# Two compressed first layers in one step, projections moved up, and an output projection that opens with the convolution's half

## The reference, cut to what matters

```python
proj = h @ w_in                       # q, six k/v parts, gate logits, b_gate, c_gate, u
k_c = rms_norm(compress(kv[0], ...)); v_c = compress(kv[1], ...)
# compress: 32-token blocks with stride 16 -> silu(blocks @ w1) @ w2; w1 is 2048 x 256
o_attn = g0 * attention(k_c, v_c) + g1 * attention(k_s, v_s) + g2 * attention(k_w, v_w)
y_conv = b_gate * short_conv(c_gate * u, conv_w)      # width 3 over tokens
mix = rms_norm(concat([o_attn, y_conv]) in groups of 64)
x = x + g1 * (mix @ w_out)
h2 = rms_norm(x) * (1 + sc2) + sh2
x = x + g2 * hier_moe(h2)             # 64 experts, two per token
```

## Time and profile before

| | |
|---|---|
| median of 3 runs | 1448.33 us (1446.87 to 1449.07) |
| profiled execution, whole time | 1447.13 us |
| its span | 1445.3 us |
| mean granted TensorE clock | 0.872 of full |
| busy: PE / PE weight loads | 1028.2 us (71%) / 532.5 us (37%) |
| busy: DVE / ACT / POOL | 457.4 us (32%) / 166.1 us (11%) / 59.1 us (4%) |
| DMA | 503.75 MB, mean 349 GB/s |

### The profile page before, as it was taken

One profiled execution on the slowest core, in us unless ns is written; L12 is line 12 of the kernel. 1 busy time (PEld: TensorE's weight loads), 2 busy tenths in 40 slices (PEclk: granted clock), 3 DMA queues, 4 the chain that ended last, 5 costly groups with the idle time before them and its releaser, 6 DMA issues.

```text
span 1445.3 us, 14719 instructions
## 1 busy us (share of the span) xinstructions
PE 1028.2 (71%) x5933; PEld 532.5 (37%) x5933; DVE 457.4 (32%) x932; ACT 166.1 (11%) x409; POOL 59.1 (4%) x94
## 2 busy tenths in 40 slices
PE   4999999999999986466465664665645646566366
PEld 1867688655455442122121221212212212122121
DVE  1255477443467361121120211212112112021121
ACT  1132222012233210000000000000000000000000
POOL 4000210011020000000000000000000000000000
PEclk9999999999999999788887887878868878788688
DMA  9946656656626579999999999999999999999996
GB/s 352 370 169 239 240 219 233 230 95 204 225 85 243 205 296 428 428 428 428 427 429 428 429 428 428 429 429 428 429 429 429 429 429 428 429 429 427 428 426 260
DMA packets 78638, 503.75 MB, mean 349 GB/s; under 512 B 5318, under 2 KB 10718, under 8 KB 54020
## 3 DMA queue, kind: packets, MB, share of 16 engines
q1 hardware_dynamic: 75872, 496.22, 83.8%
q0 software_dynamic: 2656, 6.93, 2.1%
q10 hardware_dynamic: 68, 0.02, 0.0%
HBM read 501.54 MB, written 1.61 MB: 348 GB/s over the span
## 4 chain that ended last, share of the span: by engine, by line
PE 50%; DMA 41%; DVE 4%; SPq 3%; issue 1%; ACT 0%; DVEq 0%
DMA flex<-in_w_dram 23%; DMA arena<-in_w_dram 14%; PE ps L542 11%; PE ps L531 10%; PE ps L1011 9%; PE ps L1036 7%; PE ps L986 3%; PE ps L1054 2%; DMA ring<-in_w_in_dram 2%; DMA ring<-in_w_ada_dram 2%; SPq L387 1%; PE ps L768 1%; SPq L393 1%; DVE arena L2009 1%; PE ps L663 1%
## 5 line engine op out<-in xcount | busy, mean ns | idle before, releaser
L1011 PE MATMUL ps<-ring,arena 128*32 128x512 f32 x1024 | 258.8, 663 | 97.2 <-DMA arena<-in_w_dram 94.6
L1011 PE MATMUL ps<-arena 128*32 128x512 f32 x768 | 258.3, 662 | 96.7 <-DMA flex<-in_w_dram 93.9
L1036 PE MATMUL ps<-arena 128*32 128x512 f32 x384 | 146.6, 733 | 67.0 <-DMA flex<-in_w_dram 66.3
L1036 PE MATMUL ps<-ring,arena 128*32 128x512 f32 x512 | 146.7, 736 | 65.4 <-DMA arena<-in_w_dram 64.6
L542 PE MATMUL ps<-ring,flex 128*128 128x512 f32 (+1 forms) x368 | 155.7, 579 | 0.4 <-ACT flex L1104 0.4
L531 PE MATMUL ps<-flex,ring 128*128 128x256 f32 x640 | 147.7, 388 | 3.1 <-DMA ring<-in_w_in_dram 2.4
L1011 PEld LDWEIGHTS ps<-ring,arena 128*32 128x32 f32 x1024 | 66.5, 121 | 176.1 <-issue 174.7
L531 PEld LDWEIGHTS ps<-flex,ring 128*128 128x128 f32 x640 | 122.1, 194 | 22.1 <-issue 3.0
L1011 PE MATMUL ps<-flex,arena 128*32 128x512 f32 x256 | 129.6, 665 | 0.0
L1011 PEld LDWEIGHTS ps<-arena 128*32 128x32 f32 x768 | 60.2, 120 | 176.4 <-issue 173.6
L2009 DVE TENSOR_TENSOR arena<-ps,grow 128x1024 f32<-128x1024 f32 x15 | 18.4, 1224 | 264.3 <-PE ps L1036 264.3
(11 more groups left out here) (385 smaller groups left out, 1022.8 us busy)
## 6 DMA issues: line engine op xcount, KB each, us to landing
ring<-in_w_dram SPq DMA_DIRECT2D x92, 2048.0 KB, 19.8
arena<-in_w_dram SPq DMA_DIRECT2D x69, 2048.0 KB, 24.0
flex<-in_w_dram SPq DMA_DIRECT2D x23, 2048.0 KB, 28.6
ring<-in_w_in_dram SPq DMA_DIRECT2D x17, 2048.0 KB, 10.2
ring<-in_w_ada_dram SPq DMA_DIRECT2D x14, 2048.0 KB, 8.3
ring<-in_w_ada_dram SPq DMA_DIRECT2D x8, 1024.0 KB, 17.9
ring<-in_w_out_dram SPq DMA_DIRECT2D x4, 2048.0 KB, 9.7
ring<-in_w_dram SPq DMA_DIRECT2D x16, 512.0 KB, 13.2
```

What stands on the lines that cost most here:

```text
L1011: mm = pe.matmul(ps[32 * e:32 * e + 32, g, :], xe3[:, c, 32 * e:32 * e + 32], mslot(slots[e])[:, c * W5:(c + 1) * W5], start=c == 0, stop= ...
L1036: mm = pe.matmul(ps[32 * e:32 * e + 32, 2 + n, :], actT3[:, j, 32 * e:32 * e + 32], mslot(slots[e])[:, o:o + W5], start=j == 0, stop=j == ...
```

## The change

1. Both first compression layers run in one `cmp_hidden()` at w=1. The matmuls of keys and values alternate; the keys' results go to partitions 0 to 31 and the values' to 32 to 63, so the silu is on 64x256 in place of 32x512. Both weight chunks are released at its end.
2. The convolution's projections start one step earlier: unit 0 takes the place of `cmp_hidden(0)`, units 1 to 5 stand at w=2 to 6. The shifts move from w=8 to w=7, and the routing-weight matmuls (`features_shift`) from behind the rounds to w=8. ACT's copies and DVE's products follow their units.
3. The output projection of the first 128 tokens opens with features 512 to 1023 (the convolution's half) of both its units, with the transposes of the attention half between the two, and closes with features 0 to 511. To this end ACT copies the convolution's half and DVE the attention's.

```diff
-                    unit_read(39), unit_read(40), unit_read(41), (cp_h, 1), (cp_h, 2),
+                    unit_read(39), unit_read(40), unit_read(41), (cp_h, 1), (cp_h, 1),
...
-            def cmp_hidden(kv):
-
-                chunk_in(CMP + kv)
+            def cmp_hidden():
+
+                for kv in range(2):
+                    chunk_in(CMP + kv)
                 for j in range(16):
-                    mm = pe.matmul(ps[0:32, 7, kv * 256:(kv + 1) * 256],
-                                   X5[:, kv, j, :, :].rearrange("p g n -> p (g n)"),
-                                   cview(CMP + kv)[:, j, :], start=j == 0, stop=j == 15)
+                    for kv in range(2):
+                        mm = pe.matmul(ps[32 * kv:32 * kv + 32, 7, 0:256],
+                                       X5[:, kv, j, :, :].rearrange("p g n -> p (g n)"),
+                                       cview(CMP + kv)[:, j, :], start=j == 0, stop=j == 15)
                 mm.then_inc(cp_h, 1)
...
             qk_transposes(0)
-            pe.wait_ge(cp_X, 4)
-            pe.wait_ge(misc_free, misc[0])
-            cmp_hidden(0)
+            conv_input(0)
             qk_transposes(1)
...
                 if w == 1:
-                    cmp_hidden(1)
-                if 2 <= w < 8:
-                    k, i = (w - 2) // 2, w % 2
-                    if i == 0:
-                        chunk_in(CONV + 2 * k)
-                    token_unit(hT3, i, cview(CONV + 2 * k), DC)
+                    pe.wait_ge(cp_X, 4)
+                    pe.wait_ge(misc_free, misc[0])
+                    cmp_hidden()
+                if 2 <= w < 7:
+                    conv_input(w - 1)
                 if w == 8:
+                    features_shift()
+                if w == 7:
                     pe.wait_ge(cv_w, 4)
...
+            for i in range(TI):
+                mixed_features(1, i)
+            pe.wait_ge(hta_done, 5)
+            banks = [unit_bank() for n in range(2)]
+            for n in range(2):
+                chunk_in(WO2 + n)
+                for c in range(4, DC):
+                    pe.matmul(ps[:, banks[n], :], hT3[:, c, 0:P], cview(WO2 + n)[:, c, :], start=c == 4, stop=False,
+                              skip_group_check=True)
+                if n == 0:
+                    for i in range(TI):
+                        mixed_features(0, i)
+            pe.wait_ge(htv_done, 5)
+            for n in range(2):
+                for c in range(4):
+                    mm = pe.matmul(ps[:, banks[n], :], hT3[:, c, 0:P], cview(WO2 + n)[:, c, :], start=False, stop=c == 3,
+                                   skip_group_check=True)
+                mm.then_inc(unit_done[banks[n]], 1)
...
-                if w in (4, 5):
-                    u, i = 40 + w, w % 2
+                if w in (3, 4):
+                    u, i = 41 + w, (w + 1) % 2
...
-            for i in range(TI):
-                to_hT((colB[:, 72:80], None), i, 5 + i, (2, 3))
+            for i in range(TI):
+                dve.wait_ge(xt_done, 7 + i)
+                for c in range(4):
+                    ins = dve.tensor_scalar(hT3[:, c, i * P:(i + 1) * P], ps[:, 5 + i, c * P:(c + 1) * P],
+                                            colB[:, 72 + c:73 + c], None, ALU.mult)
+                ins.then_inc(htv_done, 1)
```

More of the change, by code:

```diff
@@ L780, in _, with conv_input @@
             mm.then_inc(cp_T, 1)
+            def conv_input(j):
+                k, i = j // 2, j % 2
+                if i == 0:
+                    chunk_in(CONV + 2 * k)
+                token_unit(hT3, i, cview(CONV + 2 * k), DC)
             qk_transposes(0)
-            pe.wait_ge(cp_X, 4)
-            pe.wait_ge(misc_free, misc[0])
-            cmp_hidden(0)
+            conv_input(0)
             qk_transposes(1)
@@ L809, in attn_transposes, with features_shift @@
                 p_transposes(2 * w + g, g, fx_sc)
+            def features_shift():
+                pe.wait_ge(misc_free, misc[0])
+                pe.wait_ge(wsh_ok, 1)
+                for c in range(DC):
+                    mm = pe.matmul(ps[:, 7, 144:216], cc(C_ONE), wrs[:, c * 72:(c + 1) * 72], start=c == 0,
+                                   stop=c == DC - 1)
+                mm.then_inc(wsum_done, 1)
             pe.wait_ge(tr_free, trs[0])
@@ L885, in _, with mixed_features @@
                     mm.then_inc(cp_p, 1)
[L887 to L893, removed]
-                for i in range(TI):
[L895 to L899, removed]
+            def mixed_features(half, i):
+                pe.wait_ge(xn_done, 5 + 2 * (1 - half) + i)
+                for c in range(4):
+                    mm = pe.transpose(ps[:, (5, 2)[half] + i, c * P:(c + 1) * P],
+                                      xn3[:, i, (4 * half + c) * P:(4 * half + c + 1) * P], IDN)
+                mm.then_inc(xt_done, 1)
+            for i in range(TI):
[16 more added lines that the diff above has]
+                mm.then_inc(unit_done[banks[n]], 1)
             def x_features(i, n):
@@ L917, in logits @@
                 return mm
[L919 to L941, removed]
+            pe.wait_ge(hta_done, 6)
+            pe.wait_ge(htv_done, 6)
+            x_features(0, 0)
+            token_unit(hT3, 1, cview(WO2), DC)
+            x_features(0, 1)
+            b = unit_bank()
+            for c in range(DC):
+                if c == 4:
+                    pe.wait_ge(ld_wr, 16)
+                    logits(0, 0, 1, 0)
+                    logits(0, 1, 2, 0).then_inc(r_lg, 1)
+                    x_features(1, 0)
+                mm = pe.matmul(ps[:, b, :], hT3[:, c, P:T], cview(WO2 + 1)[:, c, :], start=c == 0,
+                               stop=c == DC - 1, skip_group_check=True)
+            mm.then_inc(unit_done[b], 1)
             logits(1, 0, 3, 0)
@@ L1282, in qk_copy, with conv_copy @@
                 trs[0] += 2
+            def conv_copy(j):
+                k, i = j // 2, j % 2
+                u = 42 + j
+                if k != 1:
+                    unit_wait(u)
+                    act.copy((cu3, None, bgt3)[k][:, i, :], ps[:, u % 2, :]).then_inc(unit_free[u % 2], 1)
             qk_copy(0)
+            conv_copy(0)
             qk_copy(1)
@@ L1287, in _ @@
             for w in range(10):
[L1288 to L1293, removed]
+                if 2 <= w < 7:
+                    conv_copy(w - 1)
                 if 0 <= w - 1 < 8:
@@ L1302, in _ @@
                 if w == 1:
[L1303 to L1304 removed]
+                    act.wait_ge(cp_h, 1)
+                    act.activation(HE[0:64, 0:256], ps[0:64, 7, 0:256], ACT.Exp, scale=-1.0).then_inc(cp_e, 1)
                 if w == 2:
@@ L1340, in _ @@
             for i in range(TI):
-                to_hT((colB[:, 72:80], None), i, 7 + i, (5, 6))
+                act.wait_ge(xt_done, 5 + i)
+                for c in range(4, DC):
+                    ins = act.activation(hT3[:, c, i * P:(i + 1) * P], ps[:, 2 + i, (c - 4) * P:(c - 3) * P], ACT.Copy,
+                                         scale=colB[:, 72 + c:73 + c])
+                ins.then_inc(hta_done, 1)
             def x_columns(i, n, c1=4):
```

17 lines of the change are left out of this document (10 added, 7 removed).

## The result

| | before | changed |
|---|---|---|
| median | 1447.6 us (4 runs, 1446.23 to 1449.07) | 1437.34 us (4 runs, 1436.97 to 1437.41) |
| ratio, 95% interval | | 0.9927 [0.9914, 0.9939] |
| span of the profiled execution | 1445.3 us | 1435.5 us |

The change gains 10.3 us; 8.5 were forecast. The fourth run of before moved its median by 0.7 us. On a second chip the same pair gave 1447.12 and 1437.33 us, 0.9934 [0.9919, 0.995].

A forecast was written before the change was run, and what follows sets the result against it. PE's progress before 489.92 us was taken to set when the byte-bound expert weight stream starts. Shorter rounds (4.7) plus earlier opening (5.0) less 1.2 gave 8.5 us: 1448.33 to 1439.8 us, range 1437.3 to 1443.5.

The forecast's parts named there:

- The block moves as one: All after 489.92 us moves as one block; the experts' region should stay 921 us within 1.
- Rival D: In the experts' region DMA keeps its own pace and the gain is waited away: no gain, 1448.3 us; chance 0.04.
- The pair: Both first layers' column groups run side by side, 64 records in 7.05 us; one layer of 7.09 us leaves PE's path.
- A: The paired layers don't run side by side, 14.2 us for the pair; gain 1.4 us, 1446.9 us; chance 0.05.
- C: Each change of column group empties the array: pair 24.3 us, kernel slower at 1457.0 us; chance 0.02.
- The start and the loads: Unit 0 begins 0.4 us earlier (0 to 0.5), its weights landing in 10.0 us; unit 2 has no DMA wait.
- Rival B: A weight chunk is late: unit 0 starts 4.4 us late, gain 4.1 us, 1444.2 us; chance 0.06.
- The clock in the gap ahead of round 0: Prediction noted the earlier trace's clock at 0.50 from about 377.6 to 381 us, 3.4 us, without a term for it.
- Round 8: At w=8, 1.90 us of routing-weight matmuls just cover the last softmax; 0.3 us counted as loss.
- The opening: Output projection opens at 465.6, not 475.31 us; low clock from PE's wait costs 0.9 us (0.4 to 2.1).
- The sum: Second unit ends at 481.4 against 489.92 us, gain 8.5: 4.7 shorter rounds, 5.0 earlier opening, less 1.2.

The follow-up runs named there:

- in series: Changed kernel with the pairing alone undone, all 16 keys' matmuls first, then the 16 of the values; 1440.53 us, ratio 0.9955.
- the wide keys' layer: Kernel before with the keys' first layer on 128 stationary columns in place of 32; 1447.8 us, ratio 1.0005.
- the filled wait: Changed kernel plus three 128x512 matmuls on constants behind the compressed attention, in PE's idle time before the convolution's transposes; 1434.4 us.
- The kernel without filler in round 8: Changed kernel with the routing-weight matmuls back behind the compressed attention; 1438.22 us.
- Without the split: Changed kernel with edit 3 (opening with the convolution's half) alone undone, both halves transposed before four whole units; 1441.96 us, ratio to before 0.9965.
- filled wait again: Second run of the changed kernel plus three matmuls on constants behind the compressed attention; 1434.27 us, ratio 0.9917.

## Why the prediction was right or wrong, step by step

The direction, the mechanism and the place were right. The size was too small by 1.6 us at the second unit's end (10.1 for 8.5), and the median, 1437.34 us, stands at the very edge of the range. In order:

- **The block moves as one: right.** From the first freed place to the end it is 921.6 us for 920.95, at 427 to 429 GB/s as before. The stretch ahead of it became 10.3 us shorter, the span 9.8. Rival D, which had this length growing by the gain, is out.
- **The pair: right.** Forecast 7.05 us, measured 7.03 for 64 records, 110 ns each; in series they take 14.86. So rivals A (14.2) and C (24.3) are out. The trace has the weight loads too, 110 ns each for 32 columns (changed kernel, 376 to 386 us: busy us, mean ns of one, idle us before):

```profile
L770 PE MATMUL ps<-ring,arena 128*32 128x256 f32 x64 | 7.1, 380 | 0.0
L770 PEld LDWEIGHTS ps<-ring,arena 128*32 128x32 f32 x64 | 3.6, 110 | 3.3 <-issue 0.3
```

  PE has no idle time in these 7.1 us and its loads are busy for 3.6 of them. The sentence on the Trainium skill's rule (TensorE: Matmul & The Clock Gate, Part 3: Packing small matmuls), that loads overlap running matmuls only where the row group differs, put an estimated 1.7 us on them; at the 110 ns of the trace it would have been 7.0 us. The trace does not agree with that rule: both groups use all rows, and nothing was added.
- **The start and the loads: right.** Unit 0 began 0.6 us sooner behind the transposes than the keys' layer had (0.4 forecast). Its weights landed 9.95 us after their issue, and unit 2 did not wait for the u weights. Rival B is out.
- **The clock in the gap ahead of round 0: the term that was missing.** I noted that it fell there in the earlier trace rows and then left it as it was, in both kernels. This execution of the changed kernel kept it. The values' layer had taken 8.17 us where the pair took 7.03, and from the first score matmul to the layer it was 1.42 us before (377.30 to 378.72) and 0.93 now (376.42 to 377.35), by the two chains:

```profile
377.30 0.56 PE ps L794 x4
```

```profile
376.42 0.49 PE ps L801 x4
```

  That is 1.14 + 0.49 = 1.6 us. Two runs put the same price on such a fall from either side: the wide keys' layer, which lacked it, had its transposes of the convolution's half 1.7 us sooner than before, and the filled wait, which had it, 1.7 us later than the changed kernel (98.4 for 96.8). Together with the start, the item at w=1 ended 2.3 us sooner where I had 0.4: 1.9 us more than forecast.
- **Round 8: mis-sized.** From there to the convolution's first transposes I had 4.3 us and the profile has 5.16, 0.9 more. I took the last softmax over from before with its 4.3 us, from 452.26 to 456.55, and said its cover was just enough. Now it takes 3.6, because DVE's wait for ACT in the middle of it shrank from 0.90 to 0.25 us. ACT's copy of an earlier transposed softmax (L1184, now L1207) stands ahead of ACT's share of the softmax; it started 1.16 us after DVE's first operation before and 0.32 us after it now. In the changed kernel:

```profile
448.76 0.28 DVE L1531 CUSTOM_DVE_ANT_0 flex<-ps,arena 128x128 f32<-128x128 f32 x1
...
452.39 0.69 DVE L1798 TENSOR_TENSOR xn<-ps,arena 128x512 f32<-128x512 f32 x1
```

  The kernel without filler in round 8 shows that no cover was needed at all. The wait of PE of 1.06 us there moved nothing: DVE's products and ACT's squares set the transposes.
- **The opening: mechanism right, clock mis-sized.** The clock fell where I said, in PE's wait ahead of the transposes. It cost 5.71 - 3.45 = 2.3 us instead of 0.9, 1.4 more, since the low stretch lasted to 466.8 and the opening had begun at 462.7. The transposes between the units took 0.87 us for the 1.1 of the sum. From the first transposes to the second unit's end it gained 2.7 us of a forecast 3.8. The filled wait, 3.70 us at a full clock, shows that it was the clock. Without the split the old wait of 3.7 us is back and the gain 2.8 to 3.0 us smaller.
- **The sum.** +1.9 (gap) + 0.9 (round 8) - 1.1 (opening) = +1.7 us beyond 8.5: the 10.1 measured at the second unit's end, within rounding.

So the step that failed is the clock's. At the opening I priced it at 0.9 us with a range that ended at 2.1, and it cost 2.3. At the gap ahead of round 0 I gave it no term and no reason, though the change put other work ahead of that gap, and it was worth 1.6 us here. The second mis-sized term is round 8 (0.9 us). The two errors of the clock have opposite signs and partly cancel, so that the sum came as near as it did is in part luck. How often the clock falls at the gap in either kernel stays open: the profiles of one kernel disagree with each other. So the 1.6 us are what this pair of profiles differs by, and no fixed property of the change. Open too is why the layers in series took 3.9 us less as a whole than their stage says.

## What to carry to other kernels

Two narrow f32 layers that both use all 128 rows belong in two column groups of one loop, where they take the time of one; and an accumulation over halves that become ready at different times should be opened with the half that is ready first. A TensorE wait of some 3 us ahead of a dense stretch cost twice here, as idleness and as a low clock behind it: throwaway matmuls that end before the wait does took the opening from 5.71 to 3.70 us. Where executions already differ ahead of the change (here by up to 3.8 us) by as much as the terms of the sum, read each profile from an anchor in front of it, and price every fall of the clock as a range at each gap, also at those that the change seems to leave alone.

## What the runs showed of the hardware

- The granted clock, once it had fallen to 0.50, stayed there for 3.4 us or 6.8 us each time between 350 and 525 us of these profiles but one, 13.6 us (filled wait again, 497.6 to 511.2). Whether it falls, and where, differs between executions of one kernel: before lost it at 377.6 in one profile and at 367.8 in another.
- It fell at 377.6 in the kernel before after two waits of only 0.78 and 0.72 us.
- The weight loads of 32 columns took 110 ns each and lay under the other column group's matmuls, although both groups use all 128 rows: 64 records of 128x256 in 7.03 us.
- The same 24 gathering records took 2.92 us at full clock, 5.46 at 0.50 throughout and 4.54 with both; the first freed place came at 146.7 us with the first and at 149.3 with the second, from the same second unit's end within 0.2 us.
- The transposes just ahead of the change began between 362.4 and 366.2 us with an equal program in front of them. The experts' region took 920.8 to 921.6 us, but for one profile of 919.6.
